# The layer stages of a two-block transformer step: when the gate row's products run, and the output product by tile

## What is computed

```python
def second_block(x, c, ...):
    for l in range(2):
        mod = silu(c) @ ada_w[l] + ada_b[l]
        sh1, sc1, ga1, sh2, sc2, ga2, sh3, sc3, ga3 = split(mod, 9)
        n = rms_norm(h, norm_g[l, 0]) * (1 + sc1) + sh1
        h = h + 0.5 * ga1 * swiglu(n, ffn_w_in[l, 0], ffn_w_out[l, 0])
        n = rms_norm(h, norm_g[l, 1]) * (1 + sc2) + sh2
        h = h + ga2 * token_mixing(n, ...)
        n = rms_norm(h, norm_g[l, 2]) * (1 + sc3) + sh3
        h = h + 0.5 * ga3 * swiglu(n, ffn_w_in[l, 1], ffn_w_out[l, 1])
    return rms_norm(h, final_norm_g)

def token_mixing(n, ...):
    ...                                  # three attention branches y_a, y_b, y_c
    merged = g_a * (y_a @ br_nsa) + g_b * (y_b @ br_dil) + g_c * (y_c @ br_fox)
    return merged @ w_out                # the output product, 1024 x 1024
```

## Time and profile before

| | us |
|---|---|
| median of three runs | 2039.82 |
| the three runs | 2040.3, 2039.82, 2037.81 |
| the profiled execution | 2040.75 |
| span of the profile | 2039.0 |
| PE busy in it | 1934.6 (95%) |
| DVE busy | 1377.2 (68%) |
| ACT busy | 987.8 (48%) |
| POOL busy | 84.9 (4%) |
| DMA | 458.42 MB, 225 GB/s on the mean |

### The profile page before, as it was taken

The page is one execution under the profiler, slowest core; times in us unless marked ns, Lnnn a source line. Parts: engine busy times, 40 slices in busy tenths (PEclk is TensorE's granted clock), DMA queues, the critical chain, the costliest instruction groups (busy, mean ns, idle before and its releaser), DMA issues.

```text
span 2039.0 us, 29874 instructions
## 1 busy us (share of the span) xinstructions
PE 1934.6 (95%) x12656; PEld 1721.1 (84%) x12656; DVE 1377.2 (68%) x1459; ACT 987.8 (48%) x1147; POOL 84.9 (4%) x107
## 2 busy tenths in 40 slices
PE   7989999999997999999998899999999999989998
PEld 3977778888887899899877899989998997779997
DVE  4889568898896877656336777768766462475444
ACT  3355457777774333444444433343335444444332
POOL 1330100000001000000000000000001000000000
PEclk9989889999998999999998999999999999899999
DMA  8555449998994786654312588658873542134454
GB/s 362 213 216 219 163 177 349 348 376 348 348 363 165 299 299 253 242 184 174 120 63 103 210 318 296 245 191 328 293 267 140 191 168 81 62 124 166 186 186 155
DMA packets 63877, 458.42 MB, mean 225 GB/s; under 512 B 7040, under 2 KB 7296, under 8 KB 8832
## 3 DMA queue, kind: packets, MB, share of 16 engines
q1 hardware_dynamic: 63744, 456.51, 59.6%
HBM read 455.43 MB, written 1.05 MB: 224 GB/s over the span
## 4 chain that ended last, share of the span: by engine, by line
issue 57%; PE 30%; DVE 7%; ACT 2%; DMA 1%; POOL 1%; DVEq 1%; POOLq 0%; ACTq 0%; SPq 0%
PE PS L359 8%; PE PS L361 8%; PE PS L360 8%; DVE acc L332 2%; DVE wlo L286 2%; ACT whi L280 1%; PE PS L1259 1%; PE PS L969 1%; DMA raw<-in_stream 1%; PE PS L1331 1%; PE PS L1343 1%; POOL Z L491 1%; DVE hlo L468 0%; PE PS L941 0%; PE PS L345 0%
## 5 line engine op out<-in xcount | busy, mean ns | idle before, releaser
L286 DVE TENSOR_TENSOR wlo<-raw,whi 128x2048 fp32r<-128x2048 f32 x282 | 646.9, 2296 | 342.3 <-ACT whi L280 337.1
L280 ACT ACTIVATE whi<-raw 128x2048 fp32r<-128x2048 f32 x282 | 538.5, 1912 | 353.7 <-PE PS L361 308.9
L359 PE MATMUL PS<-whi,hhi 128*128 128x256 f32 (+1 forms) x1568 | 507.0, 323 | 27.3 <-DVE wlo L286 12.7
L360 PE MATMUL PS<-wlo,hhi 128*128 128x256 f32 (+1 forms) x1568 | 495.4, 316 | 0.0
L361 PE MATMUL PS<-whi,hlo 128*128 128x256 f32 (+1 forms) x1568 | 495.2, 316 | 0.0
L359 PEld LDWEIGHTS PS<-whi,hhi 128*128 128x128 f32 x1568 | 306.6, 196 | 50.8 <-DVE wlo L286 14.4
L359 PE MATMUL PS<-hhi,whi 128*128 128x256 f32 x1152 | 326.7, 284 | 2.2 <-DVE mod L354 2.2
L361 PE MATMUL PS<-hhi,wlo 128*128 128x256 f32 x1152 | 326.0, 283 | 0.0
L360 PE MATMUL PS<-hlo,whi 128*128 128x256 f32 x1152 | 325.9, 283 | 0.0
L361 PEld LDWEIGHTS PS<-whi,hlo 128*128 128x128 f32 x1568 | 306.2, 195 | 17.0
L360 PEld LDWEIGHTS PS<-wlo,hhi 128*128 128x128 f32 x1568 | 306.7, 196 | 15.5
(11 more groups left out here) (398 smaller groups left out, 1786.6 us busy)
## 6 DMA issues: line engine op xcount, KB each, us to landing
raw<-in_stream SPq DMA_DIRECT2D x285, 1024.0 KB, 4.8
ada<-in_ada SPq DMA_DIRECT2D x92, 1024.0 KB, 4.9
ada<-in_stream SPq DMA_DIRECT2D x48, 1024.0 KB, 4.9
raw<-in_ada SPq DMA_DIRECT2D x3, 1024.0 KB, 15.4
xs<-in_x SPq DMA_DIRECT2D x1, 1024.0 KB, 11.5
Z<-in_ada SPq DMA_DIRECT2D x1, 1024.0 KB, 19.4
Z<-in_ctx SPq DMA_DIRECT2D x1, 1024.0 KB, 10.7
masks<-in_masks SPq DMA_DIRECT2D x2, 512.0 KB, 9.6
```

The costliest lines, as they stand in the source:

```text
L280: nc.scalar.activation(whi[:, s], src, ACT.Copy).then_inc(hi_ready, 1)
L286: nc.vector.tensor_tensor(wlo[:, s], src, whi[:, s].bitcast(F32), ALU.subtract).then_inc(lo_ready, 1)
L359: nc.tensor.matmul(out_, ah, bh, start=start, stop=False, skip_group_check=check)
L360: nc.tensor.matmul(out_, ah, bl, start=False, stop=False, skip_group_check=check)
```

## The change

It has five parts.

1. In the feed-forward stages whose gate isn't inside (both of layer 1), `gate_pe` is moved from behind the three head units of both tiles to behind the first unit of tile 0, and waits also for the second tile's `x_new` of the stage before. In the mixing it is moved from behind the six projections to behind the first. POOL makes the diagonals (`gate_pool`) ahead of its part of the norm rather than behind the last low part of the normed input.
2. In the feed-forward stages of layer 0, group 1's second unit is split: tile 0 ahead of `head_turn(0)`, tile 1 behind it. `half_sum` of the first half moves behind the first down product.
3. The output product goes by unit and tile (`out_rows`): pieces 0 and 1 are turned into banks 0 and 2, which the product of the third branch has left by then, so that WO0 for tile 0 can start on banks 4 and 5 after piece 0 alone; pieces 2 and 3 are turned behind it, into banks 6 and 7.
4. On DVE the last two gated pieces are written by tile (`last_gated`), and `split_lo(3)`, the low part of piece 0, comes ahead of `merged(2)` and `merged(3)`. ACT's `split_hi` reads the new banks.
5. On SP, in the mixing of layer 0, the second part of the second conditioning half is loaded two units later.

```diff
@@ hidden_pe
+            inside = gate_inside(k, l)
             for t in range(NT):
                 head_part(pe, 0, 0, c0, E0, (t,), lo_at(k, l))
+                if t == 0 and not inside:
+                    pe.wait_ge(*N2.x_new.at(2 * k + 1, l))
+                    gate_pe(pe, N2, k, l, 6)
                 head_part(pe, 0, 1, c0, E0, (t,))
                 if t == 0:
                     norm_pe(pe, N2, k, l, 1, xn, TB)
                 head_part(pe, 1, 0, c0, E0, (t,))
-            inside = gate_inside(k, l)
             if not inside:
-                gate_pe(pe, N2, k, l, 6)
-            head_turn(pe, 0, h0)
-            head_part(pe, 1, 1, c0, E0, range(NT))
-            if nh:
+                head_turn(pe, 0, h0)
+                head_part(pe, 1, 1, c0, E0, range(NT))
+            else:
+                head_part(pe, 1, 1, c0, E0, (0,))
+                head_turn(pe, 0, h0)
+                head_part(pe, 1, 1, c0, E0, (1,))
+            if nh and not inside:
                 half_sum(pe, v0, 1)
             if not inside:
                 pe.wait_ge(*N2.row.at(k, l))
             clear_sums(pe)
             pe_down(pe, 0, c0, E0, h0)
+            if nh and inside:
+                half_sum(pe, v0, 1)
@@ out_product is replaced
+        def out_rows(pe, c, e, w, t, parts=range(2)):
+
+            u = unit(pe, c + w, e)
+            for kk in parts:
+                ins = rows_product(u, kk, hhi[:, 2 * w + kk], hlo[:, 2 * w + kk], 4, w + kk == 0, w + kk == 4, False, (t,))
+            return ins
@@ the mixing on PE
+        MERGED_BANK = (0, 2, 6, 7)
...
                     if t:
                         ins.then_inc(unit_used, 1)
-            gate_pe(pe, N2, 1, l, 2)
+                    if t + j == 0:
+                        gate_pe(pe, N2, 1, l, 2)
...
-            for j in range(4):
+            def turn_merged(j):
                 pe.wait_ge(*B["br_out"].at(2 + j, l))
-                turn_two(mg, 2 * j, 4 + j)
+                turn_two(mg, 2 * j, MERGED_BANK[j])
+
+            turn_merged(0)
+            turn_merged(1)
+            pe.wait_ge(*B["y2_lo"].at(3, l))
+            out_rows(pe, WO0, E0, 0, 0)
+            turn_merged(2)
+            turn_merged(3)
+            pe.wait_ge(*B["y2_lo"].at(4, l))
+            out_rows(pe, WO0, E0, 1, 0, (0,))
             pe.wait_ge(*B["y2_lo"].at(6, l))
-            out_product(pe, WO0, E0, B["y_half"], lambda: norm_pe(pe, N2, 2, l, 0, xn, TB))
+            out_rows(pe, WO0, E0, 0, 1).then_inc(unit_used, 1)
+            out_rows(pe, WO0, E0, 1, 0, (1,))
+            out_rows(pe, WO0, E0, 2, 0)
+            out_rows(pe, WO0, E0, 3, 0).then_inc(*B["y_half"].up)
+            out_rows(pe, WO0, E0, 1, 1).then_inc(unit_used, 1)
+            out_rows(pe, WO0, E0, 2, 1).then_inc(unit_used, 1)
+            norm_pe(pe, N2, 2, l, 0, xn, TB)
+            out_rows(pe, WO0, E0, 3, 1).then_inc(unit_used, 1)
@@ the mixing on ACT
-                split_hi(3 + j, 4 + j, hhi[:, 2 * j:2 * j + 2])
+                split_hi(3 + j, MERGED_BANK[j], hhi[:, 2 * j:2 * j + 2])
@@ pool_layer
             for k in range(3):
+                if not gate_inside(k, l):
+                    gate_pool(pool, N2, k, l)
                 if k or l:
                     norm_pool(pool, N2, k, l)
-                pool.wait_ge(*N2.lo.at(4 * k + 3, l))
-                gate_pool(pool, N2, k, l)
+                if gate_inside(k, l):
+                    pool.wait_ge(*N2.lo.at(4 * k + 3, l))
+                    gate_pool(pool, N2, k, l)
@@ the mixing on DVE
-            for j in range(2):
+            def last_gated(j):
                 for t in range(NT):
-                    c = slice(256 * j, 256 * j + 256)
-                    nc.vector.tensor_tensor(mt2[1][:, t, c], PS[:, 2 * t, c], G[8 + j][:, t], ALU.mult)
+                    c = slice(256 * (j % 2), 256 * (j % 2) + 256)
+                    nc.vector.tensor_tensor(mt2[1][:, t, 256 * j:256 * j + 256], PS[:, 2 * t + j // 2, c], G[8 + j][:, t], ALU.mult)
+
+            last_gated(0)
+            last_gated(1)
             dve.drain()
             merged(0)
             dve.wait_ge(unit_used, E0 * 3 + (BR0 + 3))
-            gated(2, 2, 0, mt2[1])
+            last_gated(2)
             merged(1)
-            gated(2, 3, 0, mt2[1])
+            last_gated(3)
+            split_lo(3, MERGED_BANK[0], hhi[:, 0:2], hlo[:, 0:2])
             dve.drain()
             merged(2)
             merged(3)
-            for j in range(4):
-                split_lo(3 + j, 4 + j, hhi[:, 2 * j:2 * j + 2], hlo[:, 2 * j:2 * j + 2])
+            for j in range(1, 4):
+                split_lo(3 + j, MERGED_BANK[j], hhi[:, 2 * j:2 * j + 2], hlo[:, 2 * j:2 * j + 2])
             for u in range(1, 3):
                 conv_lo(dve, BR0 + u + RING, E0)
             conv_lo(dve, WO0 + RING, E0)
@@ SP, the loop over the mixing's units
-                    if l == 0 and j in (1, 5):
-                        load_half(sp, QKV_HALVES[j // 5])
+                    if l == 0 and j == 1:
+                        load_half(sp, QKV_HALVES[0])
+                    if l == 0 and j in (5, 7):
+                        load_half(sp, QKV_HALVES[1], (j // 7,))
                     load(sp, QK0 + RING + j, E0)
```

## The result

The changed kernel takes 2028.74 us (median of five runs, 2027.63 to 2030.23) beside 2039.97 for the kernel before in the same five rounds: a ratio of 0.9938, 95% interval 0.9927 to 0.9948. The forecast was 2028.6. The profiled execution is 2028.74 with a span of 2027.0.

The account below looks back on a forecast made before the run. PE, busy 1934.6 of 2039.0 us, was taken as the bound, leaving waits and clock to gain. Terms -3.6 - 5.2 - 4.5 - 6.8 + 5.0 + 3.8 = -11.3 gave 2028.6 us, range 2019 to 2035.

Parts of the forecast that it names:

- Heads: Layer 0's feed-forward stages: products fill PE's waits for h, half_out limiting the gain to 1.7 and 1.9; -3.6 us.
- Gate's products: Mixing of both layers and layer 1's second feed-forward stage: gate's products move into waits, off the path; -5.2 us.
- SP's hold: Layer 0's mixing: later conditioning load removes a visible wait of 3.95 and the slow clock behind it; -6.8 us.
- Output product: Both layers: PE waits 3.6 us for WO1's low part, queued on DVE behind the last split_lo; +2.5 per layer, +5.0.
- WO3's: Output product: PE reaches WO3 at 1125.35, before it is ready at 1125.8, and waits 0.5 us.
- Rival A: Output product gains because WO1's low part is there when PE wants it; -22.1 us, 2017.7; chance 7%.
- Rival C: Clock falls in the 3.6 us wait and stays low through the output product; +23.5 us, 2063.3; chance 7%.
- The sentence on the Trainium skill: Output product: throttled clock is the default, so the new wait costs clock in both layers; without this rule 2024.8.
- the 3.8 us behind the new wait: Output product: slow clock behind the wait for WO1's low part, 1.9 us per layer, +3.8 in all.
- the clock at the starts: Layer 1's three slow stage starts: filling the 2.2 us wait brings the clock to 1.00; -4.5 us.

Follow-up runs that it names:

- only_sp: Kernel before with part 5 alone (SP loads the second part of the second conditioning half two units later): 2034.82 us, ratio 0.9960.
- only_gate: Kernel before with part 1 alone (gate's products behind the first unit, POOL's diagonals earlier): 2032.05 us, ratio 0.9951.
- fill_starts: Kernel before, nothing moved, with 8 products of constants in each of layer 1's three slow starts: 2037.16 us, ratio 0.9977.
- wo1_first: Changed kernel with WO1's low part made on DVE ahead of the low parts of pieces 2 and 3: 2021.27 us, ratio 0.9893 to the kernel before.
- fill_output: Changed kernel with 14 unused products of constants on PE in the output product's wait of 3.86 us: 2028.01 us, ratio 0.9926.
- wo1_first_heads: Changed kernel with WO1's low part earlier and split heads in all feed-forward stages: 2018.11 us, ratio 0.9875 to the kernel before.
- only_output: Kernel before with parts 3 and 4 alone (output product by tile, split_lo(3) ahead of the merges): 2047.96 us, ratio 1.0027.
- the last two kernels: Changed kernel profiled again, 2029.09 us; and wo1_first_heads with 8 products of constants in layer 0's second feed-forward start, 2016.89 us.
- only_heads: Kernel before with part 2 alone (split heads and moved half_sum in layer 0's feed-forward stages): 2039.32 us, ratio 0.9983.

## Why the prediction came out

**The sum held because its terms did**, each in its own stretch of the table. *Heads:* -3.6 forecast, -3.61 in the trace, and with the limit named (`half_out`). *Gate's products:* in the mixing of layer 0 they can't be told from the hold's term; only_sp gives the hold 6.63 of the 8.42, which leaves 1.79 for them, where 1.70 was forecast (only_gate has 2.74 in that stretch, with the clock behind the hold changed as well). In layer 1's second feed-forward stage, where there is no hold, 3.24 less the 1.46 of fill_starts leaves 1.78, as forecast; in its first, 1.53 less 1.56 leaves nothing, as forecast. *SP's hold:* 6.63 for 6.8. *The mixing of layer 1* gave 0.47 more than forecast; by fill_starts 1.69 of its 3.67 is the clock, so the products gave 1.98 and not 1.70. *Output product:* +4.20 and +4.22 for +4.4; the wait was 3.86 where the working had 3.6, WO3's was 0.31 where it had 0.5 (its own terms add up to a weight that is ready at 1125.7, not 1125.8, so a wait of 0.36), and the clock cost 1.6 where it had 1.9. Rival A, in which WO1's low part is there in time, is the kernel wo1_first: its output product gained 0.9 per layer, where that rival's price was 1.0. Rival C's low clock was over by 1117.48 at the latest.

**Where luck was in it.** The 0.1 us between forecast and median says little: the interval of the ratio allows 10.6 to 14.9 us, and the trace is 12.0 shorter where the sum had 11.3, 0.4 of it by the output products and 0.5 by the mixing of layer 1. And two waits of the changed kernel kept their clock in both of its profiles, for which the prediction had no reason: the unfilled start of layer 0's second feed-forward stage, low in wo1_first, fill_output and wo1_first_heads, and the wait of 2.00 for h that the change opens in layer 1, low in only_gate. The prediction put the clock at both at nothing; each fall would have cost 1.5.

The sentence on the Trainium skill ("TensorE: Matmul & The Clock Gate", "What's actually happening": the throttled clock is the default, activity releases it) stood for the 3.8 us behind the new wait. The trace agrees with 1.6 per layer, 3.3 in all, by fill_output; the sum without it, 2024.8, would have been 4 us too low.

**The step with the weakest reason was the clock at the starts.** The size was right (1.53, about 1.7 and 1.46), and fill_starts shows that idle time is needed for it: with the same work and the wait filled, the clock stays. But the prediction treated the unfilled wait as slow wherever it had been slow. In the experiments the clock was low behind about half of such waits at the starts, at places that differ from kernel to kernel; in only_output two of the three starts recovered with no edit there. A change that had only shifted the stages in time could have shown the same -1.5 or its opposite. So about 4.5 of the 11 us stand on firm ground only as "no start with a filled wait was slow, 32 of 32 with the last two kernels", not as a difference of two kernels. Nor can totals of single parts be added up: by the ratios the four make 16.2 us less (3.5 + 10.0 + 8.2 - 5.5) and the whole change 12.6, with intervals of some 2 to 3 us either way on each; by the stretches of one trace each the four make 8.9 and the whole change 12.1.

**What stays open** is what decides which unfilled wait of 2.2 us lowers the clock. That it was the same in three traces of one program and another in kernels with other stages edited fits a dependence on when the wait falls; it isn't shown, since no run tested that by itself and the granted clock also varies between runs of one kernel.

## What to carry to other kernels

When products are pulled forward, look at what their next operand stands behind in the other engine's queue: here 12 matmuls ran 3 us earlier, and the whole gain and more went into the wait for a weight conversion that was left behind the pieces it no longer had to follow. A wait of 2 us on PE can cost the clock behind it on top of itself, here 1.5 to 1.7 us where it fell, and work that is moved into such a wait can then gain twice; a trace in which the clock was kept there is no proof that the next edit keeps it. Cut two traces at the same instructions and compare stretch by stretch before believing a total.

## What the runs showed of the hardware

At the stage starts, behind an unfilled wait of 2.2 us on PE, the granted clock was either 1.00 or, over the next 3.8 us, 0.55 to 0.70 (20 of 38 starts in the fourteen profiles), with nothing between 0.70 and 1.00; the low one cost 1.5 to 1.7 us. Behind a wait that products had filled down to 0.15 to 0.46 it was 1.00 in 32 of 32. Behind the waits for h, of 1.99 to 2.27, it was low in 2 of 19. Behind 3.86 us it was 0.83 or 0.84 over ten us in every output product that had this wait (changed kernel twice, only_output), and 1.00 in both that had it filled with 3.3 us of products nobody needs; but in only_heads it was 0.83 over ten us behind the short waits of the old output product too, of which the longest is 1.74. Adding 24 useless products made a kernel 4.7 us faster.
